# Head mixing: the 16 x 16 diagonal blocks of the triangular inverses move from TensorE to VectorE, by way of DMA

## Chip, core, metric

One Trainium2 chip, one of its cores. The time is that of one execution on the device, in microseconds. The kernel is one launch; all data are float32 in device memory.

## What is computed

One block of a streaming encoder for 1024 frames of width 2048: a projection in, two kinds of heads (16 RWKV-7 heads and 16 window attention heads of width 64), a projection out, and a layer of 32 experts. The change lies in the RWKV-7 heads, whose recurrence is

```
def step(state, inp):
    r_t, w_t, k_t, v_t, a_t, b_t = inp
    sa = jnp.einsum('bhvk,bhk->bhv', state, a_t)
    state = (state * w_t[:, :, None, :] + sa[..., None] * b_t[:, :, None, :]
             + v_t[..., None] * k_t[:, :, None, :])
    return state, jnp.einsum('bhvk,bhk->bhv', state, r_t)
```

The kernel does not step through the frames. It takes them in chunks of 128. Within a chunk, the frames depend on each other through a strictly triangular 128 x 128 matrix A (the scores of the vectors a against the vectors b, with the decays in them), and what the steps would do one after another is a product with the inverse of I - A. One such inverse is needed for each of 16 units: 8 chunks times the 2 heads of a pair.

## The kernel before

`project_in`, `mix_heads`, `project_out`, `route`, `experts`, `experts_over` and `finish` run one after the other. `mix_heads` loops over `PAIRS` = 8 turns, one for each pair of heads (128 channels), with all 1024 frames in it. A turn has these stages:

- preparation: three tiles of z are mixed, the low-rank products, tanh, the running sums of the decays and the norms (L617 to L782);
- scoring: 16 units, three matmuls each (L927 to L929), masked into SC on VectorE (L786). SC[:, u, 0, :] holds A of unit u;
- inversion by doubling (L787 to L797 on VectorE, L646 to L662 on ScalarE, L935 to L983 on TensorE): `LEVELS` = 7 levels, from blocks of size 1 to the full 128. Y holds the inverses of the blocks so far, in the memory of L2 (a tile of the preparation whose content is no longer needed), and X their transposes, in the memory of mix. At level lev, T = A times the odd blocks of Y (`products_t`, L941), T is masked into T1 by `copy_predicated` on VectorE (L795), and the product of X and T1 gives the new odd blocks of Y (`products_y`, L949), which ScalarE copies from PSUM (L656). `flip_y` (L962) transposes Y into X, and ScalarE copies that (L662). Level 0 is a masked transpose of A (L968) and a copy (L651). A level works in two packs of 8 units, and one level needs the Y of the level before;
- the state chain: 8 chunks one after the other (L985 to L1018), then the normalisation and the output.

Attention for the same pair of heads is spread over the turn in 12 slots (k = 0 to 11). `PLACES` says at which place of the turn a slot stands, and each engine does its part of the slot there (`attend_pe`, `attend_act`, `attend_dve`).

The order on each engine is the order of the program text; there is no scheduler. Engines wait for each other by semaphores that count up through the turns (`wait`). On SyncE (SP in the profile) a turn issues, in this order: the low-rank weights and the z tiles of the next turn (`load_lora`, `load_z`), the q, k and bias tiles of the next turn (`load_q`), and the two stores (`store`).

Ahead of the loop, the masks are loaded as floats into the memory of SC and cast to bytes on VectorE (L689, L690), and T1 is filled with blocks of the identity (L696, L699), since the masked copies only write the entries beside them.

## Time and profile before

| | us |
|---|---|
| median of three runs | 4181.4 |
| lowest and highest run | 4171.49 and 4185.65 |
| the profiled execution | 4188.65 |
| its span, first to last instruction | 4186.6 |

| engine | busy us | share of the span |
|---|---|---|
| TensorE matmul (PE) | 3608.7 | 86% |
| TensorE weight load (PEld) | 3017.2 | 72% |
| VectorE (DVE) | 1979.5 | 47% |
| ScalarE (ACT) | 1665.5 | 40% |
| GpSimd (POOL) | 293.4 | 7% |

The mean granted clock of TensorE is 0.895 of full speed. The program's first part (to about 893 us) is `project_in`; `mix_heads` follows to about 2360 us, then `project_out`, the routing from 2749 us and the experts from 2890 us. The shares are means over these parts. The profile page cuts the span into 40 slices; its rows are read with the windows and timelines of single turns, which show what each stage waits for. Everything below is from this one profiled execution.

### The profile page before, as it was taken

What the parts mean: (1) busy time and instruction counts of PE and PEld (TensorE: products, weight loads), DVE (VectorE), ACT (ScalarE), POOL (GpSimd) and SP (SyncE); (2) the same over time, 40 slices, a digit from 0 to 9 for tenths busy, and PEclk for the clock granted to TensorE, in tenths of its full rate; (3) what the DMA queues carried; (4) which work ended last, traced back from release to release, by engine and by line L of the source; (5) the groups of instructions that cost most, each with busy time, mean ns of one, the idle gap of its engine ahead of it and who ended that gap; (6) DMA issues with size and microseconds to landing.
All of it is one profiled execution on the core that took longest, in us unless ns stands there. A gap on an engine that the chain in (4) does not pass through costs nothing. (4 is left out here: it accounts for less than half of the span.)

```text
span 4186.6 us, 51511 instructions
## 1 busy us (share of the span) xinstructions
PE 3608.7 (86%) x18983; PEld 3017.2 (72%) x18983; DVE 1979.5 (47%) x2653; ACT 1665.5 (40%) x2207; POOL 293.4 (7%) x238
## 2 busy tenths in 40 slices
PE   6999999958797978879788699963999999999980
PEld 5888888847685866859577587863788888888860
DVE  3110110124435344362543323223888888888875
ACT  4111111113333333333233212131777777777761
POOL 0000000000000000000000000012111111111110
PEclk9999999977887978888688899975999999999995
DMA  3221221220101001010000423252999999999976
GB/s 126 75 75 60 75 75 60 75 78 17 40 1 40 18 23 40 1 40 13 28 23 1 171 100 130 90 157 74 346 376 381 380 377 378 380 379 384 379 277 252
DMA packets 131995, 627.50 MB, mean 150 GB/s; under 512 B 31044, under 2 KB 35396, under 8 KB 68356
## 3 DMA queue, kind: packets, MB, share of 16 engines
q1 hardware_dynamic: 122116, 591.85, 38.2%
q0 software_dynamic: 9728, 33.60, 2.0%
q8 instruction: 99, 1.62, 0.2%
q14 instruction: 52, 0.43, 0.0%
HBM read 581.12 MB, written 77.82 MB: 157 GB/s over the span
## 5 line engine op out<-in xcount | busy, mean ns | idle before, releaser
L1614 DVE TENSOR_TENSOR w_lo_e<-raw,w_hi_e 128x2048 fp32r<-128x2048 f32 x384 | 874.1, 2290 | 179.2 <-ACT w_hi_e L1553 177.3
L1553 ACT ACTIVATE w_hi_e<-raw 128x2048 fp32r<-128x2048 f32 x384 | 736.1, 1928 | 297.4 <-PE ps_y L1670 108.8
L234 PE MATMUL psA<-hn_hi,w_hi 128*128 128x512 f32 x1184 | 473.7, 400 | 6.5 <-DVE w_lo L218 6.5
L236 PE MATMUL psA<-hn_hi,w_lo 128*128 128x512 f32 x1184 | 467.4, 395 | 0.0
L235 PE MATMUL psA<-hn_lo,w_hi 128*128 128x512 f32 x1184 | 465.2, 393 | 0.0
L218 DVE TENSOR_TENSOR w_lo<-wraw,w_hi 128x2048 fp32r<-128x2048 f32 x37 | 84.8, 2293 | 711.5 <-ACT w_hi L193 711.5
L200 ACT ACTIVATE z_sb<-psA 128x512 f32<-128x512 f32 x74 | 44.2, 598 | 722.2 <-PE psA L236 722.2
L795 DVE COPY_PREDICATED T<-level_mask,psB 128x512 f32<-128x512 uint8 x128 | 91.7, 729 | 419.4 <-PE psB L941 382.2
L236 PEld LDWEIGHTS psA<-hn_hi,w_lo 128*128 128x128 f32 x1184 | 222.9, 188 | 58.3
L234 PEld LDWEIGHTS psA<-hn_hi,w_hi 128*128 128x128 f32 x1184 | 222.9, 188 | 58.0 <-DVE w_lo L218 6.7
L235 PEld LDWEIGHTS psA<-hn_lo,w_hi 128*128 128x128 f32 x1184 | 223.0, 188 | 53.1
L1165 PE MATMUL psD<-wo_hi,y_hi 128*128 128x512 f32 x512 | 201.2, 393 | 40.9 <-DVE wo_lo L1137 40.9
L941 PE MATMUL psB<-L,SC 128*128 128x64 f32 x1536 | 222.8, 309 | 0.0
L941 PEld LDWEIGHTS psB<-L,SC 128*128 128x128 f32 x1536 | 221.7, 230 | 0.0
L1668 PE MATMUL ps_y<-w_hi_e,hT_hi 128*128 128x512 f32 x512 | 214.2, 418 | 6.6 <-issue 6.6
L1668 PE MATMUL ps_g<-w_hi_e,xT_hi 128*128 128x512 f32 x512 | 204.4, 399 | 10.3 <-DVE w_lo_e L1614 10.3
L949 PE MATMUL psB<-T,mix 128*128 128x64 f32 x1536 | 206.9, 300 | 0.0
L949 PEld LDWEIGHTS psB<-T,mix 128*128 128x128 f32 x1536 | 201.3, 215 | 7.1 <-issue 7.1
L1670 PE MATMUL ps_y<-w_hi_e,hT_lo 128*128 128x512 f32 x512 | 204.0, 398 | 0.0
L1668 PE MATMUL ps_u<-w_hi_e,xT_hi 128*128 128x512 f32 x512 | 202.5, 396 | 0.0
L1669 PE MATMUL ps_y<-w_lo_e,hT_hi 128*128 128x512 f32 x512 | 202.5, 395 | 0.0
L1669 PE MATMUL ps_g<-w_lo_e,xT_hi 128*128 128x512 f32 x512 | 201.3, 393 | 0.0
(305 smaller groups left out, 6632.4 us busy)
## 6 DMA issues: line engine op xcount, KB each, us to landing
raw<-in_w_gate SPq DMA_DIRECT2D x128, 1024.0 KB, 9.8
raw<-in_w_up SPq DMA_DIRECT2D x128, 1024.0 KB, 7.5
raw<-in_w_down SPq DMA_DIRECT2D x128, 1024.0 KB, 9.3
wraw<-in_w_in SPq DMA_DIRECT2D x37, 1024.0 KB, 5.4
wo_raw<-in_w_out SPq DMA_DIRECT2D x32, 1024.0 KB, 5.0
zT<-z_sb SPq DMA_DIRECT2D x36, 512.0 KB, 2.9
y<-yk SPq DMA_DIRECT2D x8, 2048.0 KB, 9.4
z<-zT SPq DMA_DIRECT2D x26, 512.0 KB, 4.5
```

The costliest lines, as they stand in the source:

```text
L234: nc.tensor.matmul(ps[2 * b + h][:, :], w_hi[:, b, k, :], hn_hi[:, k, cols], start=k == 0, stop=False)
L235: nc.tensor.matmul(ps[2 * b + h][:, :], w_hi[:, b, k, :], hn_lo[:, k, cols], start=False, stop=False)
L236: last = nc.tensor.matmul(ps[2 * b + h][:, :], w_lo[:, b, k, :], hn_hi[:, k, cols], start=False, stop=k == KT - 1)
L795: nc.vector.copy_predicated(T1[:, lev, g % 2, :], level_mask[:, lev, :, :].rearrange("p u c -> p (u c)"), ps[T_BANK[g % 2]][:, :]).then_in ...
L941: ins = mm(o, SC[:, u, 0, :], odd_blocks(Y[:, u, :], lev), start=True, stop=True)
L949: ins = mm(ps[Y_BANK[g]][:, i * HEAD:(i + 1) * HEAD], X[:, 8 * g + i, :], T1[:, lev, g, i * HEAD:(i + 1) * HEAD], start=True, stop=True)
L1165: mm(o, y_hi[:, kk, ts], hi[:, i % 2, k, :], start=kk == 0, stop=False)
L1553: nc.scalar.activation(hi[:, s, :], raw[:, r, :], ACT.Copy).then_inc(hi_set, 1)
L1614: nc.vector.tensor_tensor(lo[:, s, :], raw[:, r, :], hi[:, s, :].bitcast(F32), ALU.subtract).then_inc(lo_set, 1)
L1668: mm(o, a_hi, hi[:, s, cols], start=start, stop=False)
L1669: mm(o, a_hi, lo[:, s, cols], start=False, stop=False)
L1670: return mm(o, a_lo, hi[:, s, cols], start=False, stop=stop)
```

## The change

Levels 0 to 3 of the doubling are taken out; together they make the inverses of the 16 x 16 blocks on the diagonal of each 128 x 128 matrix. There are 16 units with 8 such blocks (`NBB` = 8), so 128 blocks, one for each partition.

- When all scores are in SC, SyncE stores the blocks to device memory (`move_blocks`): 8 DMAs, one for each position b of a block on the diagonal, each with 16 rows of 16 units of 16 elements, so 256 pieces of 64 bytes. It waits for all 8, and loads them into AD, one block of 256 elements to a partition.
- VectorE inverts all 128 blocks together (`invert_blocks`): 17 instructions, each of which waits for the one before. Blocks of 4 by rows, then doubled to 8 and to 16. The result is in MT.
- SyncE stores MT, waits, and loads it by 8 DMAs with 64-byte pieces into the diagonal blocks of Y. GpSimd has set Y to zero before (one memset of L2, after the last operation that reads L2's old content).
- TensorE waits for those 8 DMAs and does levels 4, 5 and 6 as before, each now beginning with the transposes.
- The attention slots 1 and 2 stand at "diag out", 3 at "diag back", 4 at "level 5" (they stood at levels 0, 1, 3 and 4).
- The masks and the identities for levels 0 to 3 go. AD and MT are set to zero once, and MT gets a diagonal of ones.

```
+BASE = 4
+BB = 1 << BASE
+NBB = P // BB
+SUB = 4
...
-        masks_wide = SC[...].rearrange("p u a c -> p (u a c)")[:, 0:(LEVELS + 1) * 4 * P]
-        T1 = sb("T1", [P, LEVELS, 2, 4 * P])
+        masks_wide = SC[...].rearrange("p u a c -> p (u a c)")[:, 0:(LEVELS - BASE + 1) * 4 * P]
+        T1 = sb("T1", [P, LEVELS - BASE, 2, 4 * P])
+        AD, MT = sb("AD", [P, BB * BB + BB]), sb("MT", [P, BB * BB + BB])
+        prod, WT = sb("prod", [P, BB * BB * 2]), sb("WT", [P, BB * BB // 4])
...
-        PLACES = {"norm": (0,), "level 0": (1,), "level 1": (2,), "level 3": (3,), "level 4": (4,), "chunk 0": (5,),
+        PLACES = {"norm": (0,), "diag out": (1, 2), "diag back": (3,), "level 5": (4,), "chunk 0": (5,),
                   "chunk 1": (6,), "chunk 2": (7,), "chunk 3": (8,), "chunk 5": (9,), "chunk 6": (10,), "chunk 7": (11,)}
...
+
+                def move_blocks(turn):
+
+                    wait(sp, score_set, turn, UNITS)
+                    for b in range(NBB):
+                        at = slice(b * BB, (b + 1) * BB)
+                        sp.dma_start(a_diag[b].rearrange("u i j -> i u j"), SC[at, :, 0, at]).then_inc(diag_saved.sem, 16)
+                    wait(sp, diag_saved, turn, 16 * NBB)
+                    sp.dma_start(AD[:, 0:BB * BB], a_diag.rearrange("b u i j -> (b u) (i j)")).then_inc(diag_out.sem, 16)
+                    wait(sp, inv_step, turn, 17)
+                    sp.dma_start(m_diag.rearrange("b u j i -> (b u) (j i)"), MT[:, 0:BB * BB]).then_inc(inv_saved.sem, 16)
+                    wait(sp, inv_saved, turn, 16)
+                    wait(sp, y_zeroed, turn, 1)
+                    for b in range(NBB):
+                        at = slice(b * BB, (b + 1) * BB)
+                        sp.dma_start(Y[at, :, at], m_diag[b].rearrange("u j i -> j u i")).then_inc(diag_back.sem, 16)
...
                     load_z(turn + 1)
+                    move_blocks(turn)
                     wait(sp, slot_filled, turn, TT)
                     wait(sp, biased, turn, TT)
                     load_q(turn + 1)
                     store(turn)
                     sp.sem_inc(out_free, 1)
+                move_blocks(PAIRS - 1)
...
+                    wait(pool, ops_set, turn, 4)
+                    pool.sem_inc(seen, 1)
+                    nc.gpsimd.memset(L2[:, :, :].rearrange("p a c -> p (a c)"), 0.0).then_inc(y_zeroed.sem, 1)
...
-                    for lev in range(LEVELS):
+                    attend(attend_act, act, turn, "diag out")
+                    attend(attend_act, act, turn, "diag back")
+                    for lev in range(BASE, LEVELS):
+                        for g in range(GROUPS):
+                            wait(act, x_done, turn, (lev - BASE) * GROUPS + g + 1)
+                            nc.scalar.activation(X[:, 4 * g:4 * g + 4, :].rearrange("p u c -> p (u c)"), ps[X_BANK[g]][:, :], ACT.Copy).then_inc(x_set.sem, 1)
                         attend(attend_act, act, turn, f"level {lev}")
...
+                        for g in range(PACKS):
+                            wait(act, y_done, turn, through(lev, g + 1))
+                            nc.scalar.activation(odd_blocks(Y[:, 8 * g:8 * g + 8, :].rearrange("p u c -> p (u c)"), lev),
+                                                 ps[Y_BANK[g]][:, :].rearrange("p (m b) -> p m b", b=1 << lev), ACT.Copy).then_inc(y_set.sem, 1)
...
+                a, m = at(AD, SUB), at(MT, SUB)
+                n = BB // SUB
+                rows = m[:, :, 0:SUB * BB].rearrange("p d (j k) -> p d j k", k=BB)
+                link(v.tensor_copy(m[:, :, 1:2], a[:, :, BB:BB + 1]))
+                for i in range(2, SUB):
+                    t = prod[:, 0:n * i * i].rearrange("p (d j k) -> p d j k", d=n, j=i)
+                    link(v.tensor_tensor(t, a[:, :, i * BB:i * BB + i].unsqueeze(2).broadcast_to([P, n, i, i]), rows[:, :, 0:i, 0:i], ALU.mult))
+                    link(v.tensor_reduce(rows[:, :, 0:i, i], t, AXX, ALU.add))
+                for size in (SUB, 2 * SUB):
+                    for d in range(BB // size // 2):
+                        lo_, hi_ = 2 * d * size, (2 * d + 1) * size
+                        M3 = MT[:, 0:BB * BB].rearrange("p (i j) -> p i j", j=BB)
+                        A3 = AD[:, 0:BB * BB].rearrange("p (i j) -> p i j", j=BB)
+                        low, high = slice(lo_, lo_ + size), slice(hi_, hi_ + size)
+                        t = prod[:, 0:size ** 3].rearrange("p (i j k) -> p i j k", i=size, j=size)
+                        w = WT[:, 0:size * size].rearrange("p (j i) -> p j i", i=size)
+                        wide = lambda x, ax: x.unsqueeze(ax).broadcast_to([P, size, size, size])
+                        link(v.tensor_tensor(t, wide(A3[:, high, low], 2), wide(M3[:, low, low], 1), ALU.mult))
+                        link(v.tensor_reduce(w.rearrange("p j i -> p i j"), t, AXX, ALU.add))
+                        link(v.tensor_tensor(t, wide(M3[:, high, high].rearrange("p k i -> p i k"), 2), wide(w, 1), ALU.mult))
+                        link(v.tensor_reduce(M3[:, low, high].rearrange("p j i -> p i j"), t, AXX, ALU.add))
...
+                nc.vector.memset(AD[:, :], 0.0).then_inc(zeros_set, 1)
+                nc.vector.memset(MT[:, :], 0.0).then_inc(zeros_set, 1)
+                dve.wait_ge(zeros_set, 6)
+                nc.vector.memset(MT[:, :].rearrange("p (i c) -> p i c", c=BB + 1)[:, :, 0:1], 1.0).then_inc(zeros_set, 1)
                 for b in range(2):
-                    for u in range(4):
-                        nc.vector.tensor_copy(T1[:, 0, b, tile(u)], ident[:, :]).then_inc(zeros_set, 1)
-                    for lev in range(1, LEVELS):
+                    for lev in range(BASE, LEVELS):
                         for u in range(8):
-                            nc.vector.tensor_copy(T1[:, lev, b, u * HEAD:(u + 1) * HEAD].rearrange("p (m b) -> p m b", b=1 << lev),
+                            nc.vector.tensor_copy(T1[:, lev - BASE, b, u * HEAD:(u + 1) * HEAD].rearrange("p (m b) -> p m b", b=1 << lev),
                                                   odd_blocks(ident[:, :], lev)).then_inc(zeros_set, 1)
-                dve.wait_ge(zeros_set, 4 + 8 + later * 16)
...
-                    for lev in range(LEVELS):
-                        for g in range(PACKS if lev else GROUPS):
+                    attend(attend_dve, dve, turn, "diag out")
+                    wait(dve, diag_out, turn, 16)
+                    invert_blocks(dve, turn)
+                    attend(attend_dve, dve, turn, "diag back")
+                    for lev in range(BASE, LEVELS):
+                        for g in range(PACKS):
                             wait(dve, t_done, turn, through(lev, g + 1))
...
-                        wait(pe, y_set, turn, 2 * (g + 1) if lev == 1 else through(lev - 1, g + 1))
+                        if lev > BASE:
+                            wait(pe, y_set, turn, through(lev - 1, g + 1))
...
-                    for g in range(GROUPS):
-                        if g >= 2:
-                            wait(pe, t_set, turn, g - 1)
-                        for i in range(4):
-                            ins = nc.tensor.transpose(ps[T_BANK[g % 2]][:, tile(i)], SC[:, 4 * g + i, 0, :], ident[:, :])
-                        ins.then_inc(t_done.sem, 1)
-                    attend(attend_pe, pe, turn, "level 0")
-                    for lev in range(1, LEVELS):
+                    attend(attend_pe, pe, turn, "diag out")
+                    attend(attend_pe, pe, turn, "diag back")
+                    wait(pe, diag_back, turn, 16 * NBB)
+                    for lev in range(BASE, LEVELS):
 
                         for g in range(PACKS):
-                            flip_y(lev - 1, 2 * g)
-                            flip_y(lev - 1, 2 * g + 1)
-                            if lev > 1:
-                                products_t(lev, g)
-                        if lev == 1:
-                            for g in range(PACKS):
-                                products_t(lev, g)
+                            flip_y(lev, 2 * g)
+                            flip_y(lev, 2 * g + 1)
+                            products_t(lev, g)
                         attend(attend_pe, pe, turn, f"level {lev}")
                         for g in range(PACKS):
```

TensorE, from the end of scoring. Before, level 0, its transposes, level 1 and so on (L968: transposes of A, L962: `flip_y`, L941: T, L443, L419, L421: attention):

```order
L968 MATMUL psB<-ident_b,SC 128x128 x16
L397 ISA
L443 MATMUL psC<-kT,qT 128x192 x2
L962 MATMUL psB<-ident_b,T 128x128 x8
L397 ISA
L962 MATMUL psB<-ident_b,T 128x128 x4
L397 REGISTER_ALU
L962 MATMUL psB<-ident_b,T 128x128 x4
L941 MATMUL psB<-L,SC 128x64 x16
```

After, the last attention matmul that stands there, the wait for the blocks, and level 4 (L1024: `flip_y`, L1004: T, L1011: the product with X):

```order
L452 MATMUL psC<-kT,qT 128x192 x2
L406 ISA
L1024 MATMUL psB<-ident_b,L 128x128 x8
L1004 MATMUL psB<-L,SC 128x64 x8
L1024 MATMUL psB<-ident_b,L 128x128 x8
L1004 MATMUL psB<-L,SC 128x64 x8
L406 ISA
L1011 MATMUL psB<-T,mix 128x64 x8
```

Between scoring and the first transposes of Y, TensorE now has three attention slots and nothing else.

VectorE, after, from the end of the attention slots 1 and 2 (L523 is their last instruction) into the inversion:

```order
L523 TENSOR_SCALAR nmx<-mx 128x2
L722 COPY MT<-AD 128x4
L406 ISA
L725 TENSOR_TENSOR prod<-AD,MT 128x16
L406 REGISTER_ALU
L726 TENSOR_REDUCE MT<-prod 128x4x2
L406 REGISTER_ALU
L725 TENSOR_TENSOR prod<-AD,MT 128x36
L406 REGISTER_ALU
L726 TENSOR_REDUCE MT<-prod 128x4x3
```

The inversion stands where the ten masked copies of levels 0 to 3 stood (L795), behind two attention slots.

SyncE, after, in the loop: the new DMAs between the last z tile and the q tile of the next turn.

```order
L549 DMA z<-zT 128x1024
L406 ISA
L570 DMA a_diag<-SC 16x16x16 x8
L406 ISA
L572 DMA AD<-a_diag 128x256
L406 ISA
L574 DMA m_diag<-MT 128x256
L579 DMA L<-m_diag 16x16x16 x8
L406 ISA x2
L560 ISA
L560 DMA qT<-zT 128x1024
```

Before, the q tile followed the z tiles.

## Rows read from the trace of the kernel before

**Rows 1.** Timeline of VectorE: start us, us, engine, line, operation; the scoring evictions of turns 0 and 1

```profile
977.59 9.96 DVE L786 COPY_PREDICATED SC<-score_mask,psB 128x512 f32<-128x512 uint8 x16 [3.37 <-PE psB L929]
...
1154.96 9.91 DVE L786 COPY_PREDICATED SC<-score_mask,psB 128x512 f32<-128x512 uint8 x16 [3.48 <-PE psB L929]
```

**Rows 2.** Timeline of TensorE's matmuls, turn 0; levels 1, 2, 4 and the state chain

```profile
997.50 6.92 PE L941 MATMUL psB<-L,SC 128*128 128x64 f32 x32
...
1013.03 1.91 PE L962 MATMUL psB<-ident_b,L 128*128 128x128 f32 x8
1014.73 3.52 PE L941 MATMUL psB<-L,SC 128*128 128x64 f32 x16
...
1036.34 1.04 PE L962 MATMUL psB<-ident_b,L 128*128 128x128 f32 x8
1037.22 1.90 PE L941 MATMUL psB<-L,SC 128*128 128x64 f32 x16
...
1066.71 0.44 PE L995 MATMUL psB<-Ss,AR 128*128 128x128 f32 x2
```

**Rows 3.** Windows of turn 0; the columns are named in the first row

```profile
core 0: us, PE busy (x) PEld busy (x) DVE busy (x) ACT busy (x) POOL busy (x), PEclk, DMA share, GB/s
987.50:996.50 9.00, 5.70 (x32) 4.45 (x32) 4.04 (x9) 3.46 (x6) 0.00 (x0) 0.80 0.00 1
996.50:1020.00 23.50, 23.50 (x112) 22.63 (x111) 3.62 (x7) 6.14 (x16) 0.00 (x0) 0.50 0.00 1
1020.00:1035.50 15.50, 15.50 (x137) 15.07 (x137) 4.23 (x11) 6.33 (x16) 0.00 (x0) 0.99 0.01 2
1035.50:1066.70 31.20, 30.51 (x270) 29.76 (x270) 6.75 (x16) 12.26 (x27) 0.00 (x0) 1.00 0.00 1
```

**Rows 4.** Waits: engine, line, waited for; us in total, times, longest

```profile
DVE T L795 <- PE psB L941: 382.2, 96, 10.5
```

**Rows 5.** Windows: the same stretch of the second and of the last turn

```profile
1173.90:1197.50 23.60, 23.60 (x113) 22.74 (x112) 3.62 (x7) 6.32 (x16) 0.00 (x0) 0.50 0.00 1
...
2238.90:2262.50 23.60, 23.60 (x113) 22.73 (x111) 3.63 (x7) 6.30 (x16) 0.00 (x0) 0.50 0.00 1
```

**Rows 6.** Timeline of VectorE, attention slot 2 of turn 0

```profile
1006.26 0.56 DVE L485 SCALAR_TENSOR_TENSOR S<-psC,bias 128x384 f32<-128x384 f32 x1 [0.97 <-PE psC L443]
1006.97 0.55 DVE L510 TENSOR_REDUCE mx<-S 128x2 f32<-128x384 f32 x1 [0.15 <-DVE S L485]
1007.56 0.16 DVE L512 TENSOR_TENSOR mx<-mx,sink_now 128x2 f32<-128x2 f32 x1
1007.76 0.17 DVE L514 TENSOR_SCALAR nmx<-mx 128x2 f32<-128x2 f32 x1
```

**Rows 7.** Timeline of SyncE's DMA issues (SPq), turn 0

```profile
949.85 0.52 SPq L545 DMA_DIRECT2D wa_w<-in_w_lora_up  x1
950.89 0.51 SPq L546 DMA_DIRECT2D wa_w<-in_a_lora_up  x1
...
952.90 1.41 SPq L540 DMA_DIRECT2D z<-zT  x3
1084.12 0.33 SPq L551 DMA_DIRECT2D qT<-zT  x1
1084.73 1.13 SPq L553 DMA_DIRECT2D kT<-zT  x2
```

**Rows 8.** DMA issues of the whole run: times, KB each, median us to landing

```profile
z<-zT SPq DMA_DIRECT2D x26, 512.0 KB, 4.5
...
wa_w<-in_w_lora_up SPq DMA_DIRECT2D x8, 32.0 KB, 2.1
...
zT<-z_sb SPq DMA_DIRECT2D x1, 128.0 KB, 1.9
...
table<-empty SPq DMA_DIRECT2D x1, 70.5 KB, 18.9
...
slots_o<-table SPq DMA_DIRECT2D x1, 22.5 KB, 3.0
```

**Rows 9.** Groups by line and form: busy us, mean ns of one, idle before

```profile
L849 DVE TENSOR_TENSOR gT<-ER,gT 128x512 f32<-128x512 f32 x16 | 11.1, 692 | 0.5
...
L699 DVE COPY T<-ident_b 128x64 f32<-128x64 f32 x96 | 10.0, 188 | 0.0
...
L1534 POOL MEMSET xg<- 128x2048 f32 x1 | 1.8, 1804 | 3.5 <-POOLq L51 3.5
```

**Rows 10.** Timeline of VectorE ahead of the loop

```profile
903.99 0.43 DVE L689 CAST score_mask<-SC 128x512 uint8<-128x512 f32 x1 [9.61 <-DMA SC<-in_level_mask]
904.33 2.02 DVE L690 CAST level_mask<-SC 128x3584 uint8<-128x3584 f32 x1
...
915.40 4.99 DVE L699 COPY T<-ident_b 128x64 f32<-128x64 f32 x48
920.30 0.63 DVE L696 COPY T<-ident_b 128x128 f32<-128x128 f32 x4
```

76 lines of the change are left out of this document (36 added, 40 removed).

## The prediction

> **What bounds the kernel now.** I went from the page to the stages: its second part shows where the time lies (head mixing is slices 9 to 23 of 40), then a table of windows over one turn of head mixing, then the engines' timelines of that turn. One turn lasts 177.4 us, from the first scoring eviction at 977.59 to the next one at 1154.96 [rows 1], and there are 8 turns. Scoring ends at 987.55 (977.59 + 9.96), the first transpose of level 4 starts at 1036.34, and the state chain starts at 1066.71 [rows 1, 2]. So the inversion of the 16 triangles takes 79.2 us of 177.4 us; levels 0 to 3 are **48.8 us** of it and levels 4 to 6 are **30.4 us**. The windows show who is the bound: from 996.5 to 1066.7 TensorE is busy 69.5 of 70.2 us, and VectorE and ScalarE wait for it [rows 3]; the longest VectorE wait in this part of the kernel is for the T products, 382 us over 96 waits [rows 4]. DMA is idle throughout (0 to 2 GB/s) [rows 3]. The reader should also see the granted clock: 0.50 (1.2 GHz) for the whole of 996.5 to 1020.0, with TensorE busy 23.50 of 23.50 us, and 1.00 (2.4 GHz) after it [rows 3]. The same 16 T products take 3.52 us at the low level and 1.90 us at the full one, eight transposes 1.91 and 1.04 us [rows 2]. The low stretch stands at the same place of all 8 turns (the second and the last are shown, [rows 5]). Half of it, some 11.8 us a turn, is lost to the clock, and all of that lies in the levels that are removed.
>
> **What is removed.** Levels 0 to 3 on TensorE, VectorE and ScalarE: 48.8 us a turn, all of it on the path. The three attention slots that stood in them (k = 1, 2, 3) are not removed; they move into the time in which TensorE and VectorE would wait for DMA. Their VectorE part is some 2.1 us each (1006.26 to 1007.93, with 0.97 us of waiting ahead of some slots, [rows 6]). Slots 1 and 2 (about 5 us together) lie beside the first DMAs (7.8 us, below) and slot 3 beside the last ones, so I cost them at nothing. Without that cover they would cost 2 to 5 us a turn.
>
> **What is added, a serial chain:**
> (a) Eight DMAs out, 256 pieces of 64 bytes each. SP issues its DMAs at distances of 0.47 to 0.6 us in a turn (three in 1.41 us, two in 1.13 us), with 1.04 us as the largest [rows 7]. Eight at 0.5 us: the last leaves 3.5 us after the first. Small transfers land 1.9 to 2.1 us after issue, and one with 1,920 pieces of 12 bytes after 3.0 us [rows 8]. I take 2.1 us for the last one, since each DMA has 256 pieces only: **5.6 us** (lower end 3.3 + 1.9 = 5.2; upper end 18.9 us, the landing of the table's 6,016 small pieces into memory, which also waited behind other loads).
> (b) AD back in, 128 rows of 1 KB: **2.1 us** [rows 8].
> (c) The inversion on VectorE, 17 instructions, each waiting for the last. Linked small ones follow each other in 0.20 us (1007.56 to 1007.76, [rows 6]), a copy of 64 elements takes 0.19 us, 512 elements of a two-input operation 0.69 us, and a reduction of 384 elements 0.55 us [rows 9]. Five tiny ones at 0.20, eight with 64 elements at 0.24, four with 512 elements at 0.74: 1.0 + 1.9 + 3.0 = **5.9 us** (5 to 8; strided and repeated operands have no row here, and I take them at the rate of plain ones).
> (d) M out: 2.0 us. (e) Eight DMAs into Y: 3.5 + 2.1 = 5.6 us. (f) Five hand-overs by semaphore between SP, VectorE and TensorE at some 0.1 us: 0.5 us.
> Sum: 5.6 + 2.1 + 5.9 + 2.0 + 5.6 + 0.5 = **21.7 us**, bounds 19.7 us (the lower ends) and 30 us (each DMA 1.0 us to issue, the largest distance, which makes a group 9.1 us, and 7 us on VectorE).
>
> On SP the chain sits between the z loads and the q loads. The z loads of a turn are issued 25 us before scoring ends (952.90), the q loads at 1084.12, after the state chain has begun [rows 7]; nobody waits for either. The zeroing of L2 on GpSimd costs 1.8 us for the same shape [rows 9], starts once AR is written and is done before scoring ends: nothing.
>
> **The clock.** TensorE has next to nothing to do during the chain, so levels 4 to 6 start at the low level, where before they ran at 1.00 throughout [rows 3]. How long it stays low is the open cost. From below: level 2 begins with the same sequence (transposes, T products, transposes, T products) and the clock was full 7 us after its first transpose (1013.03 to 1020) [rows 2, 3]: half of that is 3.6 us. From above: the whole low stretch of 23.5 us again, 11.8 us [rows 5]. What decides between them is where the transposes fall, and with another turn length that will differ between turns. I take **7 us**, near the middle.
>
> **Once, ahead of the loop:** the masks shrink from 1,792 to 768 KB (1 MB less at about 400 GB/s, 2.6 us, and VectorE waits for it), their cast from 3,584 to 1,536 columns saves 1.1 of 2.02 us, and 56 of 104 copies into T go (4.99 + 1.1 us); three small memsets add 0.8 us [rows 10]. VectorE is what the others wait for there: 2.6 + 1.1 + 6.1 - 0.8 is **9 us** saved.
>
> **Sum.** Per turn 48.8 - 21.7 - 7 = 20.1 us, times 8 is 161 us, plus 9 is **170 us**. The profiled execution took 4188.65 us, so it becomes 4019 us; the median of the runs is 7.3 us below the profiled one, which gives **4012 us**.
>
> **Rivals.**
> 1. *The small pieces cost more*, but the chain still overlaps: 30 us in place of 21.7. Then 48.8 - 30 - 7 = 11.8 us a turn, 94 + 9 = 103 us, and 4078 us. For it: no row has pieces of 64 bytes in a loop, and SP's distances reach 1.04 us. Against it: 1,920 pieces in one DMA landed in 3.0 us [rows 8].
> 2. *Slower than before: the DMAs do not overlap.* If the eight of a group land one after another, at 2.1 to 2.4 us each, a group takes some 18.9 us, which is also the landing of the table [rows 8]. The chain is then 18.9 + 2.1 + 5.9 + 2.0 + 18.9 + 0.5 = 48.3 us, and with 7 us of clock each turn loses 6.5 us: 52 - 9 = 43 us slower, 4224 us. The place is the wait for diag_saved and that for diag_back; it turns to a loss when a group takes more than 15.6 us. Against it: three z loads of 512 KB leave SP within 1.41 us and land 4.5 us after their issue [rows 7, 8], so neighbours do overlap. One rule speaks against this change: the Trainium skill's page "DMA: Bandwidth & Descriptors" says under Specifications that below 512 bytes the DMA engines do read-modify-write, and under "Anatomy of one DMA" that each DMA has a fixed cost of about 2 us. By its 2 us the four steps in series hold 8 us of fixed cost, where my rows give 8.3 (2.1 + 2.1 + 2.0 + 2.1), so the sum stays; how much 64-byte pieces lose no run here shows.
> 3. *The clock is back after 3.6 us of loss each turn, or sooner.* Then 48.8 - 21.7 - 3.6 = 23.5 us a turn, and 197 us in all with the 9: 3984 us. For it: level 4 opens with transposes; against it: before, 15.5 us of products and attention at full occupation (997.50 to 1013.03) passed without a rise [rows 2, 3].
> 4. *The gain is eaten*: a chain of 36.8 us and 11.8 us of clock leave 0.2 us a turn, 11 us in all with the 9, and the time is within 0.3% (12.5 us, what a measurement of this kernel can tell) of the old one.
>
> **Chances.** Forecast (3995 to 4055) 0.53; clock early, 3984 and below, 0.15; dearer pieces, 4055 to 4130, 0.20; eaten 0.05; slower 0.07. So faster 0.88, same 0.05, slower 0.07. The range for 8 in 10 takes in the forecast and both neighbours: best case 48.8 - 19.7 - 3.6 = 25.5 us a turn, 213 us in all, 3968; on the other side the chain of 30 us with 9.7 us of clock, 82 us in all, 4100. I set 3960 to 4100.
>
> **What would show it.** In the new profile: the eight issues spaced 0.5 us, the AD load issued some 5.7 us after the last scoring eviction, the 17 VectorE steps in 6 us, the first transpose of level 4 about 22 us after scoring ends; granted clock 0.50 at that transpose and 1.00 within 7 to 24 us; from it to the state chain 37 us instead of 30.4; turns of 157 us. A group of eight that lasts over 10 us would make the chain wrong; a clock that is low until the state chain would make the 7 us wrong, and then low matmuls in the state chain too.

## The result, and the profile after

| | before | after |
|---|---|---|
| median, us | 4177.7 (4 runs) | 4042.4 (4 runs) |
| lowest and highest run, us | 4171.5 and 4185.7 | 4011.3 and 4064.9 |
| the profiled execution, us | 4188.65 | 4064.9 |
| its span, us | 4186.6 | 4063.1 |
| granted clock, mean of the profiled run | 0.895 | 0.869 |

The ratio of the times is 0.9661, 95% interval 0.9628 to 0.9694: the kernel became 135 us faster by the medians. The forecast was 170 us. Two things stand out before any detail: the runs of the new kernel lie 54 us apart, those of the old one 14 us, and the mean clock of TensorE fell. (The spread is the weaker sign: beside the three sets of experiments the old kernel was run again, and there its runs lay 29, 15 and 39 us apart.)

The profiled executions differ by 123.5 us in span. This table splits that by the stages that the prediction named. Each number is a sum over turns, read from the timelines as in [rows 1, 2]; "chain" runs from the last scoring eviction to the first transpose of level 4, "levels" from there to the state chain, "rest" from the state chain to the next scoring.

| us gained (+) or lost (-), all turns | forecast | profiled runs |
|---|---|---|
| levels 0 to 3 gone, chain added | 8 x 27.1 = +217 | 8 x 48.85 - 165.0 = +226 |
| levels 4 to 6, clock | -56 | 243.0 - 306.6 = -64 |
| rest of turns 0 to 6 | 0 | 618.4 - 669.5 = **-51** |
| last turn behind the inversion, and all that follows | 0 | +3 |
| ahead of the loop | +9 | +9 |
| sum | +170 | +123 |

So the three terms of the sum came out within 9 us of their size (two of them 9 and 8 us off, in opposite directions), and one that I had set to nothing is the miss. It isn't spread out. Turn by turn, in us:

| turn | 0 | 1 | 2 | 3 | 4 | 5 | 6 | 7 |
|---|---|---|---|---|---|---|---|---|
| chain | 21.6 | 20.5 | 20.6 | 20.4 | 20.6 | 20.3 | 20.5 | 20.5 |
| levels 4 to 6 | 34.3 | 33.8 | 39.8 | 39.8 | 39.8 | 39.7 | 39.6 | 39.9 |
| rest | 86.5 | 87.0 | 86.9 | 86.8 | **114.6** | **114.4** | **93.4** | |
| rest before | 88.3 | 88.3 | 88.5 | 88.3 | 88.3 | 88.4 | 88.4 | |

The chain itself, turn 0, timelines of SP, VectorE and TensorE (start us, us, engine, line, operation, count, and in brackets the idle time ahead with its releaser):

```profile
978.20 3.79 SPq L570 DMA_DIRECT2D a_diag<-SC  x8
...
982.20 0.17 DVE L523 TENSOR_SCALAR nmx<-mx 128x2 f32<-128x2 f32 x1
...
983.22 0.34 SPq L572 DMA_DIRECT2D AD<-a_diag  x1
...
986.25 0.17 DVE L722 COPY MT<-AD 128x4 f32<-128x4 f32 x1 [3.89 <-DMA AD<-a_diag]
...
989.46 0.69 DVE L736 TENSOR_TENSOR prod<-AD,MT 128x512 f32<-128x512 f32 x1
...
990.91 1.02 DVE L738 TENSOR_TENSOR prod<-MT,WT 128x512 f32<-128x512 f32 x1
...
992.68 0.34 SPq L574 DMA_DIRECT2D m_diag<-MT  x1
...
994.43 3.76 SPq L579 DMA_DIRECT2D L<-m_diag  x8
...
999.80 1.54 PE L1024 MATMUL psB<-ident_b,L 128*128 128x128 f32 x6 [13.62 <-DMA L<-m_diag]
```

Read it from the last scoring eviction, which ends at 978.17: eight issues at a mean distance of 0.47 us, AD's load issued 5.05 us after that end, VectorE starting 8.1 us after it (7.1 us in turn 1), 6.4 us for the 17 steps, the eight issues back, and TensorE released after 13.62 us of idleness. The attention slots 1 and 2 end on VectorE at 982.37, with 3.9 us to spare ahead of AD (2.1 us in turn 1, where slot 2 ends 0.7 us later and AD lands 1.0 us earlier, both from the end of scoring; 2.8 to 3.0 us in turns 2 to 7); slot 3 ends at 995.6, 4 us ahead of TensorE's start. The landings and the waits of the whole run (a landing is KB each and median us; a wait is us in total, times, longest):

```profile
a_diag<-SC SPq DMA_DIRECT2D x64, 16.0 KB, 1.7
AD<-a_diag SPq DMA_DIRECT2D x8, 128.0 KB, 2.0
m_diag<-MT SPq DMA_DIRECT2D x8, 128.0 KB, 1.7
L<-m_diag SPq DMA_DIRECT2D x64, 16.0 KB, 1.9
```

```profile
DVE T L857 <- PE psB L1004: 240.9, 48, 10.0
...
PE psB L1024 <- DMA L<-m_diag: 100.5, 8, 13.6
```

VectorE's wait for the T products is 240.9 us over 48 in place of 382.2 us over 96 [rows 4], and TensorE has a new wait: 12.6 us a turn for the blocks to come back.

Then the clock. Windows of turn 0 (its dead time, and both parts of its levels), and of turn 4, whose levels are followed by the state chain at 1655.9; the columns are those of [rows 3]:

```profile
990.00:999.00 9.00, 0.00 (x0) 0.00 (x0) 4.70 (x12) 0.00 (x0) 0.00 (x0) 0.50 0.19 29
999.80:1007.50 7.70, 7.70 (x37) 7.70 (x38) 0.73 (x1) 2.39 (x4) 0.00 (x0) 0.50 0.00 0
1007.50:1034.07 26.57, 25.88 (x227) 25.13 (x226) 6.00 (x15) 9.60 (x22) 0.00 (x0) 0.99 0.01 2
...
1616.35:1635.00 18.65, 18.65 (x89) 18.65 (x90) 1.45 (x2) 4.18 (x7) 0.00 (x0) 0.50 0.00 0
1635.00:1655.60 20.60, 19.93 (x170) 19.18 (x169) 5.28 (x14) 8.03 (x19) 0.00 (x0) 0.98 0.00 0
...
1655.90:1700.00 44.10, 44.10 (x196) 39.94 (x195) 10.53 (x48) 11.45 (x46) 0.00 (x0) 0.51 0.10 28
1700.00:1734.00 34.00, 27.66 (x113) 23.15 (x112) 12.70 (x58) 4.98 (x14) 3.27 (x2) 0.50 0.08 31
```

TensorE does nothing in the dead time, and level 4 starts at 0.50. The clock comes back 7 to 8 us after the first transpose in turns 0 and 1 and 19 to 20 us after it in the other six. That is the "7 us" of the sum; the loss measured 8.0 us a turn. But in turn 4 the clock, back since 1635.9, falls again at the very start of the state chain (1656.4) and stays at 0.50 for 78 us. Here is that boundary, TensorE's matmuls in turn 3 (no fall) and in turn 4 (fall):

```profile
1498.56 0.66 PE L1045 MATMUL psB<-nat,SC 128*128 128x64 f32 x4 [0.69 <-ACT L L685]
...
1499.33 0.39 PE L1053 MATMUL psB<-Ss,AR 128*128 128x128 f32 x2
...
1655.62 0.66 PE L1045 MATMUL psB<-nat,SC 128*128 128x64 f32 x4 [0.69 <-ACT L L685]
...
1656.39 0.63 PE L1053 MATMUL psB<-Ss,AR 128*128 128x128 f32 x2
```

The same instructions with the same gap of 0.69 us, in which TensorE waits for ScalarE's last copy of Y. After the gap the pair of L1053 takes 0.39 us in one turn and 0.63 us in the other. The kernel before has this gap too, in each turn, and no turn of its profile fell there. The stretch ahead of the gap doesn't tell the two turns apart either. From the return of the clock to the gap, turn 3 and then turn 4:

```profile
1478.95:1497.80 18.85, 18.85 (x165) 18.17 (x164) 5.29 (x14) 6.83 (x17) 0.00 (x0) 1.00 0.00 0
1635.95:1654.90 18.95, 18.95 (x165) 18.23 (x164) 5.28 (x14) 6.83 (x17) 0.00 (x0) 1.00 0.00 0
```

### The profile page after: what moved, and what is told of

Its sections match the earlier page's. It is cut to its first block and busy times, and to the rows that moved or that the text cites. A ratio compares the mean times of both kernels' runs of the same rounds, so it can differ in the third digit from the quotient of the medians.

```text
span 4063.1 us, 47176 instructions
## 1 busy us (share of the span) xinstructions
PE 3415.6 (84%) x16935; PEld 2826.9 (70%) x16935; DVE 1964.5 (48%) x2656; ACT 1568.2 (39%) x2031; POOL 312.3 (8%) x246
## 3 DMA queue, kind: packets, MB, share of 16 engines
q1 hardware_dynamic: 159236, 595.01, 39.9%
## 5 line engine op out<-in xcount | busy, mean ns | idle before, releaser
L234 PE MATMUL psA<-hn_hi,w_hi 128*128 128x512 f32 x1184 | 465.0, 393 | 6.5 <-DVE w_lo L218 6.5
L1220 PE MATMUL psD<-wo_lo,y_hi 128*128 128x512 f32 x512 | 201.1, 393 | 0.0
L1221 PE MATMUL psD<-wo_hi,y_lo 128*128 128x512 f32 x512 | 200.7, 392 | 0.0
L1724 PE MATMUL ps_g<-w_hi_e,xT_lo 128*128 128x512 f32 x512 | 200.6, 392 | 0.0
L1724 PE MATMUL ps_u<-w_hi_e,xT_lo 128*128 128x512 f32 x512 | 200.1, 391 | 0.0
L1723 PE MATMUL ps_u<-w_lo_e,xT_hi 128*128 128x512 f32 x512 | 199.3, 389 | 0.0
```

What stands on the lines that cost most here:

```text
L234: nc.tensor.matmul(ps[2 * b + h][:, :], w_hi[:, b, k, :], hn_hi[:, k, cols], start=k == 0, stop=False)
L1220: mm(o, y_hi[:, kk, ts], lo[:, i % 2, k, :], start=False, stop=False)
L1221: ins = mm(o, y_lo[:, kk, ts], hi[:, i % 2, k, :], start=False, stop=kk == KT - 1)
L1723: mm(o, a_hi, lo[:, s, cols], start=False, stop=False)
L1724: return mm(o, a_lo, hi[:, s, cols], start=False, stop=stop)
```

## The theories

**Theory A.** Three costs, each with its own remedy: the issue distance on SP's queue (0.47 us a DMA), the low clock in levels 4 to 6 (TensorE idle during the chain), and the low clock in the state chain (set off at the 0.69 us gap). The last one is the missing amount. **Rivals:** the low state chains are noise of the chip that any kernel has; the dead time itself causes both falls; the pieces of 64 bytes, not the issues, set the chain.

The dummy work of the experiments is one helper on TensorE. It transposes the identity into a PSUM bank that holds nothing at that point:

```
def keep_busy(n, bank):
    for i in range(n):
        nc.tensor.transpose(ps[bank][:, tile(i % 4)], ident[:, :], ident[:, :])
```

## Experiment 1: the gap ahead of the state chain filled

```
+                    keep_busy(6, 0)
                     wait(pe, y_set, turn, through(LEVELS - 1, PACKS))
```

> The changed kernel with six transposes of the identity, whose result nobody reads, on TensorE between the last products of level 6 and its wait for ScalarE's last copy of Y. In the profile of the changed kernel TensorE idles 0.69 us there in each of the 8 turns; at that gap the granted clock fell to 0.50 in turns 4 and 5 and stayed low through the whole state chain (114.5 us from the state chain to the next scoring, against 86.8 in other turns), and in turn 6 for 13 us. Theory A: the gap after a stretch of 64-column products is what lets the clock fall, where it falls badly in time. Then no turn loses its state chain, every turn is some 157 us or less, and the span is about 57 us below that of the profiled changed kernel: 4005 to 4015 us in every run, with little scatter (the changed kernel has 4011 to 4065). Rival B: the gap has nothing to do with it (the products alone, or the chip, bring the clock down): then runs scatter as before, 4010 to 4065, and low state chains are still seen.

**Measured:** 4002.3 us (3997.5 to 4006.2), ratio 0.9573 (0.9536 to 0.9609). TensorE at the same boundary of turn 4, and the first 50 us of the state chain from there, of this kernel and (second row) of the kernel after:

```profile
1654.74 0.82 PE L934 MATMUL psB<-ident_b 128*128 128x128 f32 x6
1655.59 0.66 PE L1049 MATMUL psB<-nat,SC 128*128 128x64 f32 x4
...
1656.36 0.39 PE L1057 MATMUL psB<-Ss,AR 128*128 128x128 f32 x2
```

```profile
1656.10:1706.00 49.90, 42.54 (x306) 35.84 (x306) 23.65 (x109) 16.31 (x60) 3.27 (x2) 0.90 0.14 46
```

```profile
1655.90:1706.00 50.10, 50.10 (x224) 45.94 (x224) 11.92 (x56) 12.29 (x49) 1.64 (x1) 0.50 0.09 25
```

In all seven turns the rest takes 86.6 to 86.9 us; chain and levels are what they were (20.5 to 21.5; 34.3, 33.7, then 39.7 to 39.8). The spread fell from 54 us to 9 us. Six transposes, 0.8 us of work that nobody needs, are worth 40 us: without the gap no state chain falls, and the dead time alone, which is still there, doesn't bring it.

## Experiment 2: TensorE kept busy while the blocks are away

```
                     attend(attend_pe, pe, turn, "diag back")
+                    keep_busy(56, 1)
+                    wait(pe, inv_saved, turn, 16)
+                    keep_busy(34, 1)
                     wait(pe, diag_back, turn, 16 * NBB)
```

> The changed kernel with TensorE kept at work during the DMA chain: 56 transposes of the identity after the attention slots, and 34 after the store of the inverses has landed; nobody reads their results. Nothing else is changed. Theory A: the 8.0 us a turn by which levels 4 to 6 are longer than before (33.8 to 39.8 us against 30.4) are the low clock at their start, so they come back to 30.4 to 31.5 us: 50 to 64 us less, if the transposes end before the blocks are back (they take 13.5 us where the clock rises after 7 us, and the wait is 13.6 us; 19 us if it stays low, which would cost 5 us a turn). Rival B: the levels are longer for another reason (the later start of ScalarE's copies, the level 5 slot): they stay at 34 to 40 us, and the time is that of the changed kernel. State chains at the low clock may still occur here, 26 us each.

**Measured:** 3966.7 us (3943.0 to 3988.5), ratio 0.9487 (0.9427 to 0.9547). Turn 1: the dummy transposes, then windows of the dead time and of levels 4 to 6:

```profile
1134.69 12.40 PE L934 MATMUL psB<-ident_b 128*128 128x128 f32 x90
1148.82 1.09 PE L1027 MATMUL psB<-ident_b,L 128*128 128x128 f32 x8 [1.73 <-DMA L<-m_diag]
```

```profile
1136.00:1141.00 5.00, 5.00 (x36) 5.00 (x35) 4.62 (x12) 0.00 (x0) 0.00 (x0) 0.72 0.00 0
1141.00:1148.80 7.80, 5.94 (x53) 5.46 (x51) 2.51 (x9) 0.00 (x0) 0.00 (x0) 1.00 0.24 35
1148.82:1179.24 30.42, 29.73 (x261) 28.98 (x262) 6.75 (x16) 11.77 (x26) 0.00 (x0) 1.00 0.01 1
```

The levels take 30.42 or 30.43 us in every turn, as they did before the change. The chain is 21.3 to 22.1 us, some 1 us longer in turns 1 to 7. The dummies don't hold it up: they end before the blocks have landed, 1.73 us in turn 1. The inversion starts 7.9 to 8.2 us after scoring in all turns, where the kernel after has that in turn 0 only and 7.0 to 7.2 us in the others; AD's load is issued at the same moment (5.05 us) and lands later, and why is not shown. The profiled run had no low state chain (rest 85.6 to 87.3), though the gap is open; the 45 us between the runs leave open whether that holds for each of them. The gain over the kernel after, 76 us, lies above the 50 to 64 us expected for the levels, since the profile after had lost three state chains in whole or in part. And not all of the spread need lie in the loop: in this profile the router's products behind the loop ran at the low clock, 388 ns each, where the profile after has 299 ns (256 of them; their busy time is 51.8 against 33.7 us).

## Experiment 3: both groups of eight issued from two queues

```
-                    for b in range(NBB):                     (SyncE, both groups)
+                    for b in range(0, NBB, 2):
...
+                    wait(act, score_set, turn, UNITS)         (ScalarE)
+                    for b in range(1, NBB, 2):
+                        at = slice(b * BB, (b + 1) * BB)
+                        act.dma_start(a_diag[b].rearrange("u i j -> i u j"), SC[at, :, 0, at]).then_inc(diag_saved.sem, 16)
                     attend(attend_act, act, turn, "diag out")
                     attend(attend_act, act, turn, "diag back")
+                    wait(act, inv_saved, turn, 16)
+                    (the same for Y<-m_diag)
```

> The changed kernel with every second one of the 8 + 8 small DMAs issued by ScalarE instead of SyncE. Theory A: each group is bound by the issue (8 in 3.8 us, 0.54 us apart with the gap), not by the 64-byte pieces: each group gets 1.5 to 1.9 us shorter, the chain goes from 20.5 to 17 to 17.5 us, and 24 to 30 us are saved in 8 turns. Rival B: the pieces or the landing bound the group: the group stays at 5.0 and 5.4 us, and the time does not move. State chains at the low clock may hide either, 26 us each, so the chain's own length in the trace decides.

**Measured:** 3970.3 us (3968.2 to 3988.0), ratio 0.9494 (0.9459 to 0.9529). The chain is 18.7 to 18.9 us, 1.75 us less and not 3 to 3.5 us. Turn 1, from the end of scoring at 1129.31:

```profile
1129.34 1.82 SPq L570 DMA_DIRECT2D a_diag<-SC  x4
1129.35 1.87 ACTq L679 DMA_DIRECT2D a_diag<-SC  x4
...
1132.64 0.34 SPq L572 DMA_DIRECT2D AD<-a_diag  x1
...
1134.78 0.56 DVE L494 SCALAR_TENSOR_TENSOR S<-psC,bias 128x384 f32<-128x384 f32 x1 [2.93 <-PE psC L452]
...
1136.35 0.16 DVE L731 COPY MT<-AD 128x4 f32<-128x4 f32 x1
...
1144.51 1.79 SPq L579 DMA_DIRECT2D L<-m_diag  x4
```

AD's load is issued 1.7 us earlier (3.33 us after scoring, not 5.05), but the inversion starts 7.04 us after scoring, as late as in the kernel after (7.06 in its turn 1), and with no idle time ahead of it: VectorE is still at attention slot 2. That slot came late because ScalarE had to issue four DMAs ahead of slot 1's exponentials, and TensorE's next products stand behind them. The slots, which I had costed at nothing, had 2.1 us to spare in turn 1 and 2.8 to 3.0 us in turns 2 to 7, and the edit used that up (VectorE has no idle time there in any turn). Only the group back gave its 1.8 us. (The rest of the 72 us against the kernel after is clock: in this profile the levels took 33.9 to 34.2 us in five turns and no state chain was low to its end: the clock fell at the gap in turns 2, 5 and 7 and came back in them, and the rests were 97.1 and 90.0 at worst.)

## Experiment 4: the chain left out

```
-                    move_blocks(turn)
-                    wait(dve, diag_out, turn, 16)
-                    invert_blocks(dve, turn)
-                    wait(pe, diag_back, turn, 16 * NBB)
+                    wait(pe, y_zeroed, turn, 1)
```

> The changed kernel without the move of the blocks and without their inversion (the 18 DMAs and the 17 VectorE instructions are left out; TensorE waits for the zeroed Y only, so the inverses have zero blocks on their diagonals). It prices the chain by itself. Theory A: level 4 starts some 6 to 8 us after scoring ends, behind the attention slots, instead of 20.5, and at the full clock or soon on it: 13 us and 4 to 8 us of clock less a turn, 140 to 170 us in all, about 3870 to 3900 us. Rival B: the low clock is not due to the idle time of the chain: then levels 4 to 6 stay at 34 to 40 us, and only 13 us a turn are saved, about 3940 us.

**Measured:** 3860.8 us (3856.2 to 3862.6), ratio 0.9235 (0.9201 to 0.9269). The first transpose of level 4 comes 7.9 to 8.4 us after scoring, held up by the attention slots alone. So of the chain's 20.5 us some **12.6 us** a turn, 101 us in all, is what the DMAs and VectorE's inversion cost beyond the work that stands there anyway. That is also the most that a better way of fetching and inverting the blocks could take off the chain itself; the clock comes on top. This kernel, whose inverses have zero blocks on their diagonals, is 182 us faster than the kernel after and lies below the 3870 us expected: the profiles differ by 101 us in the chain, 41 us in the levels and 67 us in the rests, and the expectation had no low state chains in it. The levels still took 31.4 to 34.4 us: even 8 us with little matmul work cost clock.

## Experiment 5: the second slot moved behind the inversion

This takes experiment 3 and changes one line, to test the reading of its trace:

```
-        "diag out": (1, 2), "diag back": (3,)
+        "diag out": (1,), "diag back": (2, 3)
```

> The kernel with the odd-numbered DMAs of both groups issued by ScalarE, and now also attention slot 2 moved from the place ahead of the inversion to the place behind it, so that one slot stands there ahead of the inversion and two behind it. Theory A (with two queues the first group ends 1.7 us earlier, but the inversion didn't start earlier, 7.03 us after the last scoring eviction against 7.06 us, because VectorE was still at slot 2, which ScalarE's issues had delayed): with slot 2 gone the inversion starts 5.3 to 5.6 us after the last scoring eviction, and the first transpose of level 4 comes at 17.0 to 17.4 us instead of 18.8: 1.5 us a turn, 12 us, 3958 us, give or take the 15 us by which low state chains differ. Rival B (the landing of AD is late for another reason, such as the DMAs of both queues finishing together as late as before): inversion still at 7.0 us, 18.8 us, 3970 us. Rival C (two slots behind the inversion are no longer covered by the DMAs back): inversion earlier, but the first transpose at 20 us or later.

**Measured:** 3996.2 us (3970.0 to 4023.0), ratio 0.954 (0.9503 to 0.9578). Turn 1, from the end of scoring at 1126.96:

```profile
1130.26 0.34 SPq L572 DMA_DIRECT2D AD<-a_diag  x1
...
1132.27 0.17 DVE L731 COPY MT<-AD 128x4 f32<-128x4 f32 x1 [2.77 <-DMA AD<-a_diag]
...
1144.72 1.54 PE L1033 MATMUL psB<-ident_b,L 128*128 128x128 f32 x6 [1.76 <-DMA L<-m_diag]
```

The inversion starts 5.3 us after scoring, with VectorE waiting for AD again, and the chain is 17.4 to 17.8 us (18.4 in turn 0). The reading held. The time did not follow: 26 us more than experiment 3 where 12 us less was expected. The profile (4023 us, the highest of the four runs) shows where it is: one state chain low to the end (turn 6, rest 114.5), three others in part (92.4, 93.3, 93.3), and levels of 39.6 to 40.0 us in five turns. **A chain that is a microsecond shorter was swamped by which turns the clock fell in.**

## Experiment 6: twice as many DMAs, the same pieces

```
-                        sp.dma_start(a_diag[b].rearrange("u i j -> i u j"), SC[at, :, 0, at]).then_inc(diag_saved.sem, 16)
+                        for us in (slice(0, UNITS // 2), slice(UNITS // 2, UNITS)):
+                            sp.dma_start(a_diag[b, us].rearrange("u i j -> i u j"), SC[at, us, 0, at]).then_inc(diag_saved.sem, 16)
                         (the group back in the same way)
```

The expectation says four units in each half; it is eight of the 16.

> The changed kernel with each of the eight DMAs out and of the eight back split in two, four units each: 16 issues in a group instead of 8, the same bytes in the same 64-byte pieces. Theory A (a group costs its issues on SP's queue, 0.47 us each, and the pieces cost nothing that is seen): each group 3.8 us longer, the first transpose of level 4 at 28.0 us after the last scoring eviction instead of 20.5; 7.5 us a turn, 60 us: 4042 + 60 = 4102 us, 4090 to 4125 with the low state chains. Rival B (a group costs its pieces, or one landing, and issue is hidden): 20.5 to 21.5 us, 4042 us. Rival C (several transfers at a time disturb each other): over 30 us, over 4130 us.

**Measured:** 4112.0 us (4092.4 to 4130.0), ratio 0.9845 (0.9798 to 0.9892). SP's queue in turn 1:

```profile
1137.25 7.46 SPq L571 DMA_DIRECT2D a_diag<-SC  x16
...
1155.98 7.42 SPq L581 DMA_DIRECT2D L<-m_diag  x16
```

Sixteen issues take 7.46 us where eight take 3.78, and the chain is 27.5 us instead of 20.5: 3.5 us more for each group, 70 us more in the median. With half the bytes in each DMA and the pieces unchanged, a group costs its issues. What pieces cost shows in the landings of this run, with 128 pieces in a DMA in place of 256:

```profile
a_diag<-SC SPq DMA_DIRECT2D x128, 8.0 KB, 1.5
L<-m_diag SPq DMA_DIRECT2D x128, 8.0 KB, 1.7
```

Half the pieces land 0.2 us sooner (1.7 and 1.9 us before), against 3.5 us for the issues. The prediction cited the Trainium skill ("DMA: Bandwidth & Descriptors", Specifications) for the read-modify-write below 512 bytes. Such pieces stand in both groups, and at 16 KB a DMA their landing, 1.7 and 1.9 us, is no longer than that of AD's 1 KB rows (2.0 us). But that load carries 128 KB, eight times the bytes, so a loss per byte is not excluded; it is only too small at this size to matter for the chain.

## Experiment 7: how much of what was removed was clock

The kernel before, with dummy transposes where TensorE waits in level 0:

```
+                    keep_busy(12, 1)
                     wait(pe, score_set, turn, UNITS)
...
+                        if g == 2:
+                            keep_busy(8, 3)
...
                     attend(attend_pe, pe, turn, "level 0")
+                    keep_busy(6, 3)
...
+                            if lev == 1 and g == 1:
+                                keep_busy(20, 3)
```

> The kernel before, with dummy 128x128 transposes on TensorE where it waits in level 0 (12 ahead of the last scores, 8 ahead of the third group of level 0's transposes, 6 behind the attention slot, 20 ahead of the second flip of level 1). Nothing else is changed. It asks how much of the 48.8 us a turn that the change removed was work and how much was the low clock: before, TensorE is granted 0.50 for 23.5 us of levels 1 and 2 in each turn, busy all the time. Theory A (the removed levels cost 37 us of work and 11.8 us of low clock, which the change took away with them): 11.8 us a turn less, 8 turns, 4184 - 94 = 4090 us, 4080 to 4110 with what the dummy transposes themselves delay. Rival B (the removed levels are bound by VectorE's and ScalarE's evictions there, so that the clock costs little): 4160 to 4184 us.

**Measured:** runs of 4105.7, 4118.7, 4188.9 and 4190.7 us, two groups for which one ratio says little. The profiled one is that of 4118.7 us. Windows of turn 1, levels 1 and 2 and what follows, and of the start of turn 7's state chain at 2219.65:

```profile
1161.70:1185.20 23.50, 23.50 (x211) 22.88 (x210) 6.05 (x12) 9.89 (x26) 0.00 (x0) 1.00 0.01 1
...
2215.00:2220.00 5.00, 4.31 (x38) 4.18 (x37) 0.85 (x2) 1.19 (x2) 0.00 (x0) 0.98 0.00 0
2220.00:2225.00 5.00, 5.00 (x26) 5.00 (x25) 0.43 (x3) 0.56 (x2) 0.00 (x0) 0.50 0.00 0
```

In place of 112 matmuls at 0.50 [rows 3], 23.5 us now hold 211 at 1.00, and levels 0 to 3 take 36.8 us instead of 48.85 in every turn: **12 us of each turn were the low clock**, the 11.8 us of the prediction. The work that the change removed was 36.8 us, in place of which stands a chain of 20.5 us. And here the kernel before falls at the same gap: in turn 7 for 51 us, and in turns 1 and 3 for 7 us (rests of 91.8 and 90.9 us in place of 88.3). So the low state chain needs neither the DMAs nor the dead time.

## Experiments 8 and 9: the gap in the kernel before

Experiment 7 with the gap filled as in experiment 1:

> The kernel before with the dummy transposes in level 0 and levels 1, as in the run that took 4105.7 to 4190.7 us, and now with six more over the 0.69 us gap ahead of the state chain. It asks whether the spread of that run, 85 us, was the low state chain (its profiled turn 7 ran the state chain at 0.50 from 2220 us on, 24 to 26 us lost). Theory A: no state chain at 1.2 GHz any more; all turns alike at 177.5 - 11.1 = 166.4 us or less, 4175 - 8 x 11.1 = 4086 us, 4078 to 4095, runs within 12 us of one another. Rival B (the spread has another cause, such as dummy transposes that delay the scores in some runs): still 4100 us and more in some runs.

**Measured:** 4105.3 us (4091.3 to 4114.0), ratio 0.9803 (0.9765 to 0.9842). The spread is 23 us in place of 85, and the turns are 164.8 to 166.8 us (before 177.4); the profile has no fall at the gap any more. The median is 19 us above the expectation, and the profile (4113.8 us) has that amount behind the loop. The router's products, of this kernel first and then of the kernel before (busy us, mean ns):

```profile
L1304 PE MATMUL ps_l<-rw,xT_r 128*128 128x36 f32 x256 | 51.8, 388 | 0.0
```

```profile
L1294 PE MATMUL ps_l<-rw,xT_r 128*128 128x36 f32 x256 | 34.0, 300 | 0.0
```

They ran at the low clock, as in experiment 2: 18 us outside head mixing, in a stage that the prediction says nothing about. What makes the clock low there in two of the profiles is not shown.

The kernel before with the gap filled and nothing else:

> The kernel before with nothing but six dummy transposes over the 0.69 us gap ahead of the state chain. In its profiled run every state chain began and stayed at 1.00. Theory A (before never paid for this gap, so the low state chains are a cost that came with the change): no difference beyond 4 us from before, 4171 to 4188 us. Rival B (before paid for it too in runs that weren't profiled): runs 10 us or more shorter than before's, 4165 us or less.

**Measured:** 4186.2 us (4172.0 to 4212.4, 10 runs) against 4185.2 us (13 runs), ratio 0.9997 (0.9967 to 1.0027). No difference: to within 0.3% the kernel before did not pay for this gap, so the low state chains came with what the change, or the dummies of experiment 7, altered ahead of it. The runs of both kernels lie some 40 us apart, gap or no gap, so that spread has another cause.

## Experiments 10 and 11: all remedies together

Experiments 1, 2 and 3 in one kernel, with 50 and 28 dummies in place of 56 and 34:

> Three edits of the earlier experiments together: six dummy transposes over the 0.69 us gap ahead of the state chain, dummy transposes on TensorE while the blocks are away (50 behind the attention slots and 28 more once m_diag is stored), and the odd-numbered DMAs of both groups issued by ScalarE. Theory A (issue pitch, low clock in the levels, low clock in the state chain are three separate costs, each with its own remedy): first transpose of level 4 at 19 to 20 us after the last scoring eviction, levels in 30.4 us, rest of a turn 86.5 us without a low state chain, so 136.5 us a turn, some 12 us a turn under the kernel with the low-clock remedy missing in the levels; against the kernel with dummy transposes alone (3966.7 us, chain 21.3 to 22.1) it saves 1.8 to 2.5 us a turn, 14 to 20 us in all: 3945 to 3955 us. Rival B (ScalarE's issues delay the attention slots and the dummy transposes behind them, so that the gains don't add): no faster than the dummy transposes alone, 3960 to 3975 us.

**Measured:** **3930.7 us** (3928.8 to 3931.8), ratio 0.9403 (0.9384 to 0.9423). All turns alike: chain 20.0, levels 30.4, rest 86.4 to 86.6, turns of 146.6 to 146.8 us. It is better than the expectation by 14 us, because the kernel it was reckoned from (experiment 2) had lost 18 us at the router's products in its profile. The chain is 1.2 us longer than with two queues alone (18.8), though the inversion starts at the same 7.0 us: here the 78 dummies end after the blocks. It beats the kernel before by 244 us and the changed one by 112 us, and its runs lie 3 us apart. With the clock kept up in both kernels, a turn is 146.6 to 146.8 us here and 164.8 to 166.8 us in experiment 8: that, 18 to 20 us a turn, is what the change is worth when the clock is taken out of the comparison (the second queue is in it; with one, in experiment 2, a turn is 147.4 to 149.5 us).

The same with 18 dummies in place of 28:

```
-                    keep_busy(28, 1)
+                    keep_busy(18, 1)
```

> The kernel with all three remedies (3930.7 us) and 18 dummy transposes instead of 28 in the second piece while the blocks are on their way back. The last of the 78 ended about 1.2 us after the blocks had landed (first transpose of level 4 at 20.0 us, against 18.8 us without dummy transposes). Theory A: the first transpose comes at 19.0 us with the clock still at 1.00 through the levels (30.4 us): 1.0 us a turn, 8 us, 3922 us, 3919 to 3926. Rival B (the dummy transposes end before the landing, and a gap of some tenths of a us lets the clock fall again): levels at 34 us or more in some turns, 3940 us and more.

**Measured:** 3939.8 us (3922.9 to 3951.5), ratio 0.9422 (0.9378 to 0.9466). No difference that can be told: the interval overlaps with the one above, and the kernel before was itself 10 us slower in the set of runs beside this one. The profiled run took 3930.3 us, two others 20 us more, and no profile shows where. Neither theory as written. The dummies of turn 1 and of turn 4:

```profile
1135.49 8.81 PE L943 MATMUL psB<-ident_b 128*128 128x128 f32 x68
...
1573.61 9.88 PE L943 MATMUL psB<-ident_b 128*128 128x128 f32 x68
```

The clock came back at about 1138 in turn 1, 2.4 us after the dummies began, and at 1578.2 in turn 4, 4.6 us after; the same 68 then last 1.1 us longer, and the chain is 19.1 us in one turn and 20.1 in the other. The levels stayed at 30.4 us. So dummy work is itself timed by the clock that it is to raise, and ten fewer save a microsecond of chain in some turns and nothing in others.

## Why the prediction came out as it did

**Right: the direction, the range, and the bound.** 4042 us against 4012 forecast, in a range of 3960 to 4100. Levels 0 to 3 were on the path in full and came off in full.

**Right: the chain.** 20.3 to 21.6 us against 21.7. The issues stand 0.47 us apart where I took 0.5. AD's load was issued 5.05 us after scoring (5.7). Landings are 1.7 to 2.0 us (2.0 and 2.1). The fixed 2 us for each DMA that the prediction took from the Trainium skill ("DMA: Bandwidth & Descriptors", "Anatomy of one DMA") lies near these, but that section describes DMAs issued by GpSimd, and these are issued by SyncE. VectorE took 6.4 us where I took 5.9: its last product, with 512 elements and one operand read transposed, takes 1.02 us instead of 0.69, which I had left to the range ("at the rate of plain ones"). In turn 1 the inversion took 0.5 us more than its term, and the DMA parts out and back 0.6 us less each, hand-overs included.

**Right, with its size: the clock in the levels.** 8.0 us a turn against 7. The trace before bounded it at 3.6 and 11.8; the measured turns take both of two values, 3.4 to 3.9 in turns 0 and 1 and 9.2 to 9.5 in the others. No turn lost 7 us. That the mean of two and six such turns comes so near is luck: what puts a turn into one group or the other I had put down to where the transposes fall, and no run shows it. The forecast turn of 157 us is what turns 2 and 3 took, 157.2 and 156.9.

**Right: the slots, the queues, the start.** Slots 1 and 2 are hidden, with 2.1 us to spare in turn 1 and 2.8 us or more in the others, and so is slot 3. Ahead of the loop 9.3 us were saved (9). One reading was off without consequence: the z loads are issued 35 us before scoring ends, and 25 us before it begins.

**Wrong: "from it to the state chain 37 us", and nothing after that.** The step that failed is the sum's silence on the state chain. I wrote that a clock that is low until the state chain would bring low matmuls there too, and so tied the one to the other; the clock was at 1.00 when the state chain began, and it fell there. Three rests of 114.6, 114.4 and 93.4 us cost 57 us in the profiled run, against which the rests of turns 0 to 3 gave back 6. Experiment 1 measures it in the medians: 40 us. With the gap filled the kernel takes 4002 us, 10 us better than forecast: the sum without this term was good, if partly by errors that offset each other.

What I should have read: before the change the clock fell in level 0, in which TensorE was still busy 5.70 of 9.00 us [rows 3] and waited for 2.25 us at most at a time. That was a sign that short waits lose the clock too, not only idle stages, and the 0.69 us gap was in the same rows: 30.51 us busy of 31.20.

**The rivals.** 1 (dearer pieces, 4078 us): fell; in experiment 6 half the pieces are worth 0.2 us of landing and eight more issues 3.5 us. Its time lies nearer to the measured one than its mechanism deserves: the profiled run was 4065. 2 (DMAs not overlapping, slower): fell; eight landings overlap in 5 us. (Its turning point, a group of 15.6 us, leaves out the 9 us ahead of the loop; with them it is 16.2 us.) 3 (clock back early, 3984): held in two turns of eight. 4 (eaten): fell.

**Open.** Why the fall at the gap takes some turns and not others, and why the kernel before was spared it. What the profiles show is this. In the seven profiles of changed kernels and of experiment 7 with the gap open, the clock fell there in 15 of 56 turns, each time 0.3 to 0.8 us after the end of the gap; in the kernel before in 0 of 8; in the five kernels with the gap filled in 0 of 40. How long the clock had been back does not decide it. In the kernel after it was back 19.0 to 19.2 us ahead of the gap in turns 4, 5 and 6, which fell, and 18.9 to 19.0 us in turns 2, 3 and 7, which didn't. In the kernel before it was 45 us, in turn 7 of experiment 7, which fell, 77 us. The runs show that the gap is needed and not what else is.

## What to carry to other kernels

When a change leaves TensorE with little to do for a while (20 us here; 8 us in experiment 4 cost clock too), the clock is part of the price. Here it was paid twice: at once where the work resumes, and later at a small gap that was harmless before. Look for such gaps on a TensorE-bound path and try what filling them with spare work gives. Cost a bundle of small DMAs by the number of issues on its queue, and before moving issues to another engine ask what stands behind them on it. Where a term of the sum is missing, compare the turns of one profile with one another before comparing means.
